# The retention loop's transposes moved ahead of its readout on TensorE, and VectorE's state update ahead of its masked scores

## The reference

```python
def retention_readout(q, k, v, log_gamma, starts):
    inner = jnp.einsum('bhncs,bhnse->bhnce', jnp.einsum('bhncd,bhnsd->bhncs', qr, kr) * dmat[None, :, None], vr)
    cross = jnp.einsum('bhncd,bhnde->bhnce', qr * xi[None, :, None, :, None], starts)
    return (inner + cross).reshape(b_, h_, t_, dv)

o = (retention_readout(q, k, v, log_gamma[0], st_f)
     + _flip_t(retention_readout(_flip_t(q), _flip_t(k), _flip_t(v), log_gamma[1], st_b)))
y = head_layer_norm(o.transpose(0, 2, 1, 3), norm_g) * jax.nn.silu(g_.astype(F32))
```

## Time and profile before

| | us |
|---|---|
| median of 3 runs | 4627.56 (4623.63 to 4630.88) |
| the profiled execution | 4623.63 |
| its span, first to last instruction | 4621.6 |
| TensorE busy in the span | 4129.4 |
| VectorE busy | 1993.7 |
| mean granted clock of TensorE, share of full speed | 0.944 |

### The profile page before, as it was taken

One profiled execution on the slowest core, in us unless ns is written; L12 is line 12 of the kernel. 1 busy time (PEld: TensorE's weight loads), 2 busy tenths in 40 slices (PEclk: granted clock), 3 DMA queues, 4 the chain that ended last, 5 costly groups with the idle time before them and its releaser, 6 DMA issues. The chain is left out here.

```text
span 4621.6 us, 74631 instructions
## 1 busy us (share of the span) xinstructions
PE 4129.4 (89%) x31948; PEld 3282.2 (71%) x31948; DVE 1993.7 (43%) x3328; ACT 1068.3 (23%) x2355; POOL 978.6 (21%) x693
## 2 busy tenths in 40 slices
PE   4898988959979899999996999989599898999996
PEld 3543677848868688888884545877488776888884
DVE  3232356554452633333335233556544435443343
ACT  2211224123330311111114222232233313110011
POOL 0100010012311433333320100100033104444440
PEclk8898999979989999999997999999799999999998
DMA  3011100010001011111111111000100010111111
GB/s 157 37 73 73 64 19 20 19 50 3 3 20 37 19 38 45 36 36 36 36 41 48 37 73 55 23 24 19 41 3 3 21 37 28 46 45 48 52 45 46
DMA packets 23288, 180.00 MB, mean 39 GB/s; under 512 B 2416, under 2 KB 2672, under 8 KB 7536
## 3 DMA queue, kind: packets, MB, share of 16 engines
q1 hardware_dynamic: 21296, 166.73, 9.9%
q10 hardware_dynamic: 1728, 9.40, 0.5%
HBM read 167.73 MB, written 8.39 MB: 38 GB/s over the span
## 5 line engine op out<-in xcount | busy, mean ns | idle before, releaser
L1111 PE MATMUL ps<-Yn_parts,ring_parts 128*128 128x512 f32 (+1 forms) x3840 | 799.4, 370 | 9.9 <-issue 8.0
L1111 PEld LDWEIGHTS ps<-Yn_parts,ring_parts 128*128 128x128 f32 x3840 | 671.1, 189 | 136.0 <-issue 8.8
L1111 PE MATMUL ps<-temp_parts,ring_parts 128*128 128x512 f32 (+1 forms) x2560 | 726.4, 369 | 17.0 <-DVE Hn_parts L2126 17.0
L645 PE MATMUL ps<-ring_parts,Xn_parts 128*128 128x256 f32 x2560 | 512.8, 296 | 74.3 <-DVE ring_parts L1707 70.0
L2077 DVE SCALAR_TENSOR_TENSOR Xn<-ps,mods,Xn 128x256 f32<-128x256 f32 (+1 forms) x360 | 250.8, 697 | 692.0 <-PE ps L1111 542.9
L2345 POOL TENSOR_TENSOR ring_parts<-ring,consts 128x2048 fp32r<-128x2048 f32 x64 | 295.7, 4620 | 1193.4 <-DMA ring<-in_ff 1193.4
L1111 PEld LDWEIGHTS ps<-temp_parts,ring_parts 128*128 128x128 f32 x2560 | 465.9, 189 | 99.5 <-DVE Hn_parts L2126 18.2
L645 PEld LDWEIGHTS ps<-ring_parts,Xn_parts 128*128 128x128 f32 x2560 | 424.8, 199 | 79.3 <-issue 72.8
L1111 PE MATMUL ps<-Hn_parts,ring_parts 128*128 128x512 f32 (+1 forms) x1280 | 472.2, 369 | 0.0
L1581 ACT ACTIVATE Yn<-ps 128x256 f32<-128x256 f32 (+1 forms) x160 | 88.7, 554 | 1257.6 <-PE ps L1111 1257.6
L645 PE MATMUL ps<-ring_parts,Hn_parts 128*128 128x256 f32 x1280 | 371.3, 290 | 0.0
(11 more groups left out here) (294 smaller groups left out, 6140.0 us busy)
## 6 DMA issues: line engine op xcount, KB each, us to landing
ring<-in_ff SPq DMA_DIRECT2D x64, 1024.0 KB, 4.8
ring<-in_ada SPq DMA_DIRECT2D x24, 2048.0 KB, 8.8
ring<-in_halves SPq DMA_DIRECT2D x30, 1024.0 KB, 4.8
Xn<-in_x ACTq DMA_DIRECT2D x1, 5120.0 KB, 27.0
Xn<-in_x SPq DMA_DIRECT2D x1, 5120.0 KB, 16.1
kept_x<-Xn SPq DMA_DIRECT2D x2, 2048.0 KB, 8.1
Xn<-kept_x SPq DMA_DIRECT2D x1, 4096.0 KB, 13.5
out_x<-Xn SPq DMA_DIRECT2D x1, 4096.0 KB, 11.7
```

What stands on the lines that cost most here:

```text
L645: m = pe.matmul(ps[:, bank, 0:256], (G_hi, H_lo)[a][:, k, t * P:(t + 1) * P], w[b][:, k, :], start=(k == 0 and part == 0), stop=(k == KT - ...
L1111: m = pe.matmul(ps[:, bank, 0:hi - lo], w[a][:, k, j * P:(j + 1) * P], x[b][:, k, lo:hi], start=(k == 0 and part == 0), stop=(k == k_n - 1 ...
```

## The change

Three moves, all in the last part of the retention loop; no arithmetic changes and no instruction that computes is added or removed.

- TensorE: the two transposes go from the end of a pass to a place between the projection and the state product. They now write bank 2, not bank 3, and wait for `normed` (and `r_o`). The state product L889 no longer waits for `yT_sb`; the readout's first matmul L909 waits for `yT_sb` in place of `r_o`, since it writes the bank that ScalarE copies the transposes from.
- ScalarE: the copy L1414 reads bank 2.
- VectorE: the state update (L1915, L1916) goes ahead of the masked scores (L1910).

```diff
@@ TensorE, retention()
+                    if s_ >= 2:
+                        pe.wait_ge(sems["normed"], nth("normed", s_ - 1))
+                        pe.wait_ge(sems["r_o"], nth("r_o", s_ - 1))
+                        for j in range(2):
+                            m = turn(ps[:, 2, j * P:(j + 1) * P], r_oc[:, s_ % 2, j * P:(j + 1) * P])
+                        m.then_inc(sems["yT_mm"], tally("yT_mm"))
                     if 1 <= s_ < NT:
                         t = ret_order[s_ - 1]
                         pe.wait_ge(sems["r_state"], nth("r_state", NT + s_ - 1))
-                        if s_ >= 3:
-                            pe.wait_ge(sems["yT_sb"], nth("yT_sb", s_ - 2))
                         pe.matmul(ps[:, 3, 0:256], r_kzs[:, 1, tile_cols(t)], r_v[:, t, :], start=True, stop=True, skip_group_check=True)\
...
                         if n_:
-                            pe.wait_ge(sems["r_o"], nth("r_o", n_))
+                            pe.wait_ge(sems["yT_sb"], nth("yT_sb", n_))
...
-                    if s_ >= 2:
-                        pe.wait_ge(sems["normed"], nth("normed", s_ - 1))
-                        pe.wait_ge(sems["r_state"], nth("r_state", NT + min(s_, NT - 1)))
-                        if s_ > NT:
-                            pe.wait_ge(sems["yT_sb"], nth("yT_sb", s_ - 2))
-                        for j in range(2):
-                            m = turn(ps[:, 3, j * P:(j + 1) * P], r_oc[:, s_ % 2, j * P:(j + 1) * P])
-                        m.then_inc(sems["yT_mm"], tally("yT_mm"))
@@ ScalarE, retention()
-                        A(Y[:, 4:6, tile_cols(ret_order[n_])], ps[:, 3, 0:256].rearrange("p (a b) -> p a b", a=2), ACT.Copy)\
+                        A(Y[:, 4:6, tile_cols(ret_order[n_])], ps[:, 2, 0:256].rearrange("p (a b) -> p a b", a=2), ACT.Copy)\
@@ VectorE, retention(): this block stood ahead of the state update and now stands behind it
                     if 0 <= s_ < NT:
                         dve.wait_ge(sems["scores"], nth("scores", s_ + 1))
                         if s_ >= 2:
                             dve.wait_ge(sems["pv"], nth("pv", s_ - 1))
                         TT(r_ps[s_ % 2], ps[:, 4:8, 0:P], r_dt, ALU.mult).then_inc(sems["probs"], tally("probs"))
```

More of the change, by code:

```diff
@@ L1905, in retention @@
                         TT(r_g[:, s_, :], r_g[:, s_, :], par["ret_g"], ALU.mult)
[L1906 to L1910, removed]
                     if 1 <= s_ < NT:
@@ L1917, in retention @@
                         dve.sem_inc(sems["r_state"], tally("r_state"))
+                    if 0 <= s_ < NT:
+                        dve.wait_ge(sems["scores"], nth("scores", s_ + 1))
+                        if s_ >= 2:
+                            dve.wait_ge(sems["pv"], nth("pv", s_ - 1))
+                        TT(r_ps[s_ % 2], ps[:, 4:8, 0:P], r_dt, ALU.mult).then_inc(sems["probs"], tally("probs"))
                     if 1 <= s_ <= NT:
```

## The result

The changed kernel is slower, as forecast, and by more than the forecast's middle: 4669.12 us (median of 5, 4663.92 to 4674.20) against 4626.64 us (median of 5), ratio 1.0093, 95% interval 1.0080 to 1.0107. Timed a second time it took 4663.82 us against 4627.09 us, ratio 1.0086 (1.0067 to 1.0106). The forecast was 4657 us with a range of 4639 to 4670. The profiled execution of the changed kernel took 4659.91 us, the shortest of its set, with a span of 4657.9 us; that of before had 4621.6 us.

What follows compares the result with a forecast made beforehand. The prediction took VectorE's queue behind GpSimd's root as the bound, 7.56 us a pass. To a base of 4623.6 or 4627.6 us it added 16 us (chain, last readouts) and 16 us (clock): 4657 us, range 4639 to 4670.

Steps and rivals of the forecast that it cites:

- What bounded the loop: Retention loop: VectorE's own queue behind GpSimd's root sets the 7.56 us pass; TensorE's wait for the state update lies beside it.
- The chain through TensorE's queue: Passes 2 to 9: `normed` to mean goes from 2.99 to 3.61 us, 0.62 us a pass, 5.0 us a layer.
- The copy's cover: Full passes: ScalarE's copy is done at t + 1.37 (t: start of `normed`), 0.23 us before the readout can start.
- The last readout: Pass 10: it waits for ScalarE's copy, starts at t + 1.37 (t: start of `normed`), costs 3.0 us once a layer.
- The clock: TensorE idles about 2.1 us a pass; six low-clock stretches a layer at 1.33 us each, 16 us in two layers.
- my sign of being wrong: Profile after: wrong if the mean follows VectorE's own instructions, passes keep 7.56 us, or stretches at 0.50 stay as few.
- The full clock holds: Rival: the longer chain in the loop without stretches at 1.2 GHz, plus 16 us, 4643.6 us; chance 0.22.
- The sum: Whole kernel: 16 us for chain and last readouts plus 16 us for the clock, taken as 4657 us.
- Nothing changes: Rival: hand-offs are shorter or TensorE's chain hides behind VectorE's list, pass stays 7.56 us, 4628 to 4634 us; chance 0.09.
- VectorE's exchange: State update ahead of masked scores on VectorE: worth nothing, as VectorE is ready at t + 3.03, before the readout's t + 3.61.
- Faster: Rival: TensorE is the bound, so its 9.9 us of idle time a layer would go, 4608 us; chance 0.04.
- Worse: Rival: nearly every pass has a 1.2 GHz stretch at 1.5 us and later projections are late, 43 us, 4671 us; chance 0.07.

Runs made afterwards that it cites:

- The kernel kept busy: The changed kernel plus 14 filler matmuls on TensorE ahead of the wait for `normed` in passes 2 to 9: 4645.87 us, ratio 1.0045 to the kernel before.

## Why the prediction was right, and where its sizes were off

*What bounded the loop.* Right. VectorE's list behind the root's wait set 7.56 us a pass, and TensorE's wait for the state update lay beside it. Taking 0.6 us off that signal's path changed nothing; filling VectorE's wait took 1.46 us off a pass (7.56 to 6.10), once TensorE's transposes no longer needed this pass's `normed`.

*The chain through TensorE's queue.* Right in kind, a little short: L1932 to mean was forecast at 3.61 us and is 3.72 to 3.73, so 0.74 us a pass and not 0.62. The difference is between transposes and state product: 0.27 us (634.40 to 634.67) where I took 0.16 from a pair of transposes followed by a projection matmul. Eight passes in two layers make 11.8 us, not 9.9.

*The copy's cover.* I gave it 0.23 us, and L913 waited for it nowhere but in pass 5 of the first layer. ScalarE's list has a weight split there, which I had not looked for:

```profile
625.05 1.90 ACT L1261 ACTIVATE ring_parts<-ring 128x2048 fp32r<-128x2048 f32 x1
626.85 0.38 ACT L1410 ACTIVATE Yn<-ps 128x256 f32<-128x256 f32 x1
```

```profile
627.37 0.67 PE L913 MATMUL ps<-temp 128*128 128x256 f32 x2 [0.60 <-DVEq L1908]
```

The split (L1261, 1.90 us) stands ahead of the copy (L1410), the projection had been late from the low clock, and L913 started 0.60 us late, as the copy ended at 627.23. The trace names another releaser, DVEq L1908, the increment behind L1907, which ended at 627.31. But the count of `r_state` that L913 needs is that of the pass before, `NT + s_ - 1`, the same that L893 had already passed at 625.74, and GpSimd's scaled queries (`r_stage`) were ready by 624.67. So what held L913 was the copy. This is the one step that is longer by 0.6 us, with TensorE's own clock at 1.00 there. In the kernel before nobody waited for this copy in time to notice.

*The last readout.* The step that was mis-sized. It was forecast at 3.0 us a layer and cost 9.47 - 4.39 = 5.1. The 3.0 were worked out at full clock, and I spread the low clock over passes 2 to 9 alone, although the last readout stands behind the longest wait of the loop, 4.57 us. L913 started at t + 1.74, not t + 1.37, and its matmuls took 3.64 us (672.75 to 676.39), not 1.94: together the 2.1 us that were missing.

*The clock.* Right in cause and nearly right in sum, wrong in its parts, so the sum came out partly by luck. I took twelve stretches on the chain at 1.33 us each, 16 us. In the first profile seven steps of passes 2 to 9 are longer by 1.6 to 2.0 us, 12.2 us in all; with the 0.6 us of the copy above that is 12.8, and the two last readouts add about 2 us each. The price was above the 0 to 1.5 us that I had bounded it by, and not because matmuls of the chain suffer more: the projection lost 1.33 us in 2.98 us of low clock (602.42 to 605.40), the readout 1.71 us in 3.68 (616.70 to 620.38, in place of 1.97), 0.45 and 0.46 us per us. What I had wrong is how long the clock stays low. I took 3.4 us from the earlier trace rows; in the changed kernel four of the seven spells last 6.8 us, such as the one from 616.70, and these cost 1.7 to 2.0 us, the three of 3.4 us 1.6. So the low clock of passes 2 to 9 lasted 37.6 us in the two layers, in seven spells; before it was 20.5 us in six. By their number alone, my sign of being wrong (stretches as few as before) nearly came true.

A low clock before the change was not quite free either. Three steps a layer are longer by 0.2 to 0.3 us, since the gate waits for a tanh, and the tanh for the late projection, as in this row:

```profile
630.47 0.42 DVE L1903 SCALAR_TENSOR_TENSOR Yn<-temp,ps 128x256 f32<-128x256 f32 x1 [0.23 <-ACT temp L1404]
```

I also wrote that the idle time of a pass, 2.1 us, rises above two of the waits that a fall followed. It is above one (1.51), and just under 2.14 and 2.38. And the stage of before has a fourth low stretch that I left out, from 663.4 us on, around a wait of 3.95 us ahead of the last transposes (665.76); of this stage's matmuls only these two fell in it.

The kernel kept busy gives 12.9 us back in the loops and 18 to 23 us in the medians. The Trainium skill, "TensorE: Matmul & The Clock Gate", section "HAM oscillation — how this bites in real kernels", asks for longer gaps than the 2.16 us of these passes before the full clock is lost. By that rule the time would have been the 4643.6 us of my rival, or some 4 us more, since the 4.57 us ahead of a last readout are long enough for it; there the trace agrees with the rule. (Before's 3.95 us in the last pass are long enough too, which my sentence on the stage's passes overlooked.) For the passes the measurement decides. In the second layer the longest gap of the loop up to its first fall is 2.41 us, and the clock fell 0.8 us behind these transposes:

```profile
2974.52 0.44 PE L664 MATMUL ps<-consts,temp 128*128 128x128 f32 x2 [2.16 <-DVE temp L1932]
```

```profile
2975.30:2982.10 6.80, 6.80 (x33) 6.20 (x33) 2.69 (x7) 1.14 (x9) 0.05 (x1) 0.50 0.01 1
```

*The sum.* 11.8 us for the chain and 10.2 us for the last readouts make 22.0; with 12.8 for the long steps (clock and copy), less the 1.5 us by which before's own steps were over 7.56, that is 33.3, the 33.3 us of the loops. The forecast had 32. The medians differ by 42.5 and 36.7 us, more than the loops of the profiled executions. The profiled executions were among the shortest of the changed kernel's; whether the rest is more falls of the clock in the others or something outside the loop, the runs don't show.

*The rivals.* "The full clock holds" did not come about, but the kernel kept busy shows nearly its time, +19 us where it had +16, with the last readouts still at the low clock. "Nothing changes" fell with the step of 8.3 us; it holds for VectorE's exchange alone. "Faster" fell because the wait that the change went for was not on the path: a signal 0.6 us earlier gave nothing. "Worse" had a low clock on nearly every pass; there were seven in sixteen.

## What to carry to other kernels

An in-order engine that waits but bounds nothing has its idle time from the length of the loop; moving its wait, or bringing the signal earlier, leaves that time as it was. Before an instruction is put ahead of others on its engine, ask what everything behind it will then wait for: here two transposes with a late operand put 3 us of matmuls on the loop of dependences, and the same two transposes with an operand one pass older cost the loop almost nothing. The place to gain was the wait of the engine that did set the pass, and what could go into it was independent work from its own list.

## What the runs showed of the hardware that I had not expected

The granted clock fell behind idle gaps of 2.16 us, and what that costs depends on where the low stretch lies. Before, 1.33 us of projection time was lost and 0.2 to 0.3 us of it reached a step; on the path after, it was 1.6 us for a stretch of 3.4 us and 1.7 to 2.0 us for one of 6.8. With 14 filler matmuls in each pass, the gaps were 0.5 us, one 0.74 and one 1.35, and the clock was 1.00 through 68 us. Two profiles of the changed kernel have the same 8.3 us steps and, in the second layer, the same three long ones; in the first layer the long ones are at different places. The loops' sum differs by 1.1 us, while the medians of two sets differ by 5.3 us.
